# Linear attention's decay levels on half tiles: scaling on VectorE alone, and a predicated copy from PSUM in place of mask product and sum

## What is computed

```python
diff = bc[:, :, :, None, :] - bc[:, :, None, :, :]
decay = jnp.exp(jnp.where(causal[:, :, None], diff, -jnp.inf))
attn = jnp.einsum('bhid,bhjd,bhijd->bhij', qc, kc, decay)
o_intra = jnp.einsum('bhij,bhje->bhie', attn, vc)
```

## Time and profile before

| | us |
|---|---|
| median of 3 runs (907.64 to 909.5) | 908.16 |
| the profiled execution | 906.52 |
| its span in the trace | 904.7 |
| PE busy | 859.0 (95%) |
| DVE busy | 649.4 (72%) |
| ACT busy | 555.5 (61%) |
| POOL busy | 350.5 (39%) |

### The profile page before, as it was taken

One profiled execution on the slowest core, in us unless ns is written; L12 is line 12 of the kernel. 1 busy time (PEld: TensorE's weight loads), 2 busy tenths in 40 slices (PEclk: granted clock), 3 DMA queues, 4 the chain that ended last, 5 costly groups with the idle time before them and its releaser, 6 DMA issues.

```text
span 904.7 us, 18066 instructions
## 1 busy us (share of the span) xinstructions
PE 859.0 (95%) x6762; PEld 837.4 (93%) x6762; DVE 649.4 (72%) x1059; ACT 555.5 (61%) x999; POOL 350.5 (39%) x324
## 2 busy tenths in 40 slices
PE   4999889999999999999999989899999999999996
PEld 3998889999899899999999878799999999999996
DVE  5987999896777798777665659957577854444542
ACT  5677778887646576665555675456645655555441
POOL 3799995435432253333110215701032243333111
PEclk9999999999999999999999999999999999999999
DMA  5655444444565366665656443245345466654741
GB/s 201 209 187 186 162 144 151 137 132 140 151 184 186 111 189 205 186 180 175 214 163 194 160 142 110 82 136 166 115 143 172 150 211 188 182 180 152 217 133 47
DMA packets 42310, 146.41 MB, mean 162 GB/s; under 512 B 4704, under 2 KB 7024, under 8 KB 42224
## 3 DMA queue, kind: packets, MB, share of 16 engines
q1 hardware_dynamic: 41472, 143.67, 50.9%
q10 hardware_dynamic: 752, 1.59, 0.5%
HBM read 144.20 MB, written 1.05 MB: 161 GB/s over the span
## 4 chain that ended last, share of the span: by engine, by line
PE 72%; DVE 11%; issue 8%; POOL 6%; ACT 3%; DMA 1%; DVEq 0%; POOLq 0%; ACTq 0%
PE px L507 22%; PE px L508 22%; PE px L509 22%; DVE wlo L1316 3%; POOL CA L1876 2%; DVE px L1375 2%; POOL att L1996 1%; PE px L549 1%; PE px L571 1%; ACT whi L843 1%; DVE sq L1331 1%; POOL wlo L1827 1%; DVE Q L1406 1%; DMA X<-xs 1%; ACT hx L870 1%
## 5 line engine op out<-in xcount | busy, mean ns | idle before, releaser
L507 PE MATMUL px<-hx,whi 128*128 128x256 f32 x1392 | 404.4, 291 | 9.2 <-DVE hx L1337 6.1
L509 PE MATMUL px<-hx,wlo 128*128 128x256 f32 x1392 | 396.6, 285 | 0.0
L508 PE MATMUL px<-hx,whi 128*128 128x256 f32 x1392 | 396.6, 285 | 0.0
L1316 DVE TENSOR_TENSOR wlo<-raw,whi 128x1024 fp32r<-128x1024 f32 x251 | 330.8, 1325 | 65.0 <-ACT whi L843 64.6
L843 ACT ACTIVATE whi<-raw 128x1024 fp32r<-128x1024 f32 x267 | 279.9, 1051 | 65.0 <-PE px L509 49.8
L507 PEld LDWEIGHTS px<-hx,whi 128*128 128x128 f32 x1392 | 269.7, 194 | 14.2 <-DVE hx L1337 7.4
L508 PEld LDWEIGHTS px<-hx,whi 128*128 128x128 f32 x1392 | 270.0, 194 | 0.4
L509 PEld LDWEIGHTS px<-hx,wlo 128*128 128x128 f32 x1392 | 269.7, 194 | 0.0
L1950 POOL TENSOR_TENSOR fx<-tt,fx 128x256 fp32r<-128x256 f32 x40 | 54.3, 1359 | 130.1 <-ACT fx L1104 130.1
L1876 POOL TENSOR_TENSOR CA<-CA,ct 128x256 f32<-128x256 f32 x90 | 85.7, 953 | 45.5 <-ACT ct L910 37.9
L508 PE MATMUL px<-fx,whi 128*128 128x256 f32 x352 | 99.6, 283 | 0.0
(11 more groups left out here) (283 smaller groups left out, 1347.0 us busy)
## 6 DMA issues: line engine op xcount, KB each, us to landing
raw<-ws SPq DMA_DIRECT2D x267, 512.0 KB, 3.7
tb<-tabs SPq DMA_DIRECT2D x16, 128.0 KB, 2.7
out<-X SPq DMA_DIRECT2D x4, 256.0 KB, 2.4
X<-xs SPq DMA_DIRECT2D x1, 512.0 KB, 4.9
X<-xs ACTq DMA_DIRECT2D x1, 512.0 KB, 5.0
msk<-lmask ACTq DMA_DIRECT2D x1, 448.0 KB, 3.5
vc<-vecs ACTq DMA_DIRECT2D x1, 320.0 KB, 7.0
ug<-pos ACTq DMA_DIRECT2D x1, 128.0 KB, 4.7
```

What stands on the lines that cost most here:

```text
L507: e.matmul(b[:, 0:S], H, xh, start=first, stop=False)
L508: e.matmul(b[:, 0:S], H, xl, start=False, stop=False)
L509: m = e.matmul(b[:, 0:S], L, xh, start=False, stop=end)
L1316: e.tensor_tensor(wlo[:, n % NSL, :], raw[:, n % NRAW, :], whi[:, n % NSL, :], ALU.subtract).then_inc(s_lov, 1)
```

## The change

`factors` on DVE is now two instructions of half the size, border minus b left of the border and b minus border right of it, so both are negative and ACT needs one exp (scale +1/16) and no absolute value. Keys are scaled only left of each border and queries only right of it, both on DVE; the queries are packed into 128x256. The products then have 64 columns (the right-half queries) instead of 128. Level 0 is as before. For the other levels a predicated copy from PSUM writes the wanted places of `at` directly, two of 128x256; mask product, `tmp` and sum go. POOL loses all its level work and gets two memsets of `kL` and of half of `go`. The mask shrinks from 7x128 to 128 + 6x64 columns.

```diff
@@ TensorE, products(n), n > 0
-                    e.wait_ge(s_ql, n)
-                    e.wait_ge(s_kl, n)
+                    e.wait_ge(s_ql, n)
-                        m = e.matmul(bs[par][:, i * P:i * P + P], k_[o:o + 64, p_, t * P:t * P + P],
-                                     q_[o:o + 64, p_, t * P:t * P + P], start=(i == 0), stop=True, skip_group_check=True)
+                            m = e.matmul(bs[par][:, i * 64:i * 64 + 64], KL[n % 2][o:o + 64, p_, t * P:t * P + P],
+                                         QLf[n % 2][o:o + 64, i * 64:i * 64 + 64], start=(i == 0), stop=True,
+                                         skip_group_check=True)
@@ TensorE, linear_out()
-                e.wait_ge(s_la, 12)
+                for par in range(2):
+                    e.wait_ge(*BANK["pr", 6, par])
@@ ScalarE, factors(n)
-                e.activation(E, E, ACT.Abs).then_inc(s_fa, 1)
-                e.wait_ge(s_fa, n)
-                e.activation(E, E, ACT.Exp, scale=-1.0 / 16).then_inc(s_fe, 1)
+                e.activation(E, E, ACT.Exp, scale=1.0 / 16).then_inc(s_fe, 1)
@@ VectorE
-                if n > 2:
-                    e.wait_ge(s_kl, n - 2)
-                e.tensor_tensor(eb[:, n % 2, :].rearrange("p (n w) -> p n w", w=2 * s), bv,
-                                bv[:, :, s - 1:s].to_broadcast([P, 512 // (2 * s), 2 * s]), ALU.subtract).then_inc(s_fs, 1)
+                e.tensor_tensor(to_first, border, first, ALU.subtract)
+                e.tensor_tensor(to_second, second, border, ALU.subtract).then_inc(s_fs, 1)
...
-                e.tensor_tensor(QLf[n % 2], gqf, eb[:, n % 2, :], ALU.mult).then_inc(s_ql, 1)
+                e.tensor_tensor(halves(KLf[n % 2], n)[0], halves(gkf, n)[0], first, ALU.mult)
+                e.tensor_tensor(QLf[n % 2][:, 0:S].rearrange("p (n w) -> p n w", w=s), halves(gqf, n)[1], second,
+                                ALU.mult).then_inc(s_ql, 1)
...
-                    e.tensor_tensor(to[:, par, :].rearrange("p (a i) -> p a i", a=4), bt, mb, ALU.mult).then_inc(
-                        BANK["pr", n, par][0], 1)
+                        to = at[:, par, :].rearrange("p (a n w) -> p a n w", a=4, w=2 * s)[:, :, :, s:2 * s]
+                        e.copy_predicated(to, mb.to_broadcast([P, 4, 64 // s, s]),
+                                          px_of["pr", n, par][:, 0:S].rearrange("p (a n w) -> p a n w", a=4, w=s)).then_inc(
+                                              BANK["pr", n, par][0], 1)
@@ GpSimd
+            for n in range(2):
+                e.memset(KLf[n], 0.0).then_inc(s_pad, 1)
...
-                e.tensor_tensor(KLf[n % 2], gkf, eb[:, n % 2, :], ALU.mult).then_inc(s_kl, 1)
...
-                    e.tensor_tensor(at[:, par, :], at[:, par, :], tmp[:, par, :], ALU.add).then_inc(s_la, 1)
```

More of the change, by code:

```diff
@@ L10 @@
 I32 = mybir.dt.int32
+U32 = mybir.dt.uint32
 ALU = mybir.AluOpType
@@ L410, in two_blocks @@
         s_pad = sem("s_pad")
[L412 to L413 removed]
+        s_fs, s_fe, s_ql, s_pr, s_dec, s_dk, s_tk, s_cu, s_go = (sem(n) for n in (
+            "s_fs", "s_fe", "s_ql", "s_pr", "s_dec", "s_dk", "s_tk", "s_cu", "s_go"))
         s_gsq, s_gsm, s_gr, s_ogt, s_gn, s_gg, s_gph, s_gpv, s_gpg = (sem(n) for n in (
@@ L705, in products @@
                         p_, t = i // 2, i % 2
-                        m = e.matmul(bs[par][:, i * P:i * P + P], k_[o:o + 64, p_, t * P:t * P + P],
-                                     q_[o:o + 64, p_, t * P:t * P + P], start=(i == 0), stop=True, skip_group_check=True)
+                        if n == 0:
+                            m = e.matmul(bs[par][:, i * P:i * P + P], gk[o:o + 64, p_, t * P:t * P + P],
+                                         gq[o:o + 64, p_, t * P:t * P + P], start=(i == 0), stop=True,
+                                         skip_group_check=True)
+                        else:
+                            m = e.matmul(bs[par][:, i * 64:i * 64 + 64], KL[n % 2][o:o + 64, p_, t * P:t * P + P],
+                                         QLf[n % 2][o:o + 64, i * 64:i * 64 + 64], start=(i == 0), stop=True,
+                                         skip_group_check=True)
                 m.then_inc(s_pr, 1)
@@ L1141, in _ @@
             e.dma_start(caus[:, :], tabs[NH]).then_inc(s_caus, 16)
-            e.dma_start(msk[:, :, :], masks.rearrange("p (l i) -> p l i", l=7)).then_inc(s_msk, 16)
+            e.dma_start(msk[:, :], masks).then_inc(s_msk, 16)
             for n, key in enumerate((("cq", 0), ("cq", 1), ("cq", 2), ("ckv", 0))):
@@ L1689, in level_add @@
                     e.wait_ge(s_msk, 16)
[L1690 to L1696, removed]
-                    e.tensor_tensor(to[:, par, :].rearrange("p (a i) -> p a i", a=4), bt, mb, ALU.mult).then_inc(
-                        BANK["pr", n, par][0], 1)
+                    mb = msk[:, 0:P].rearrange("p (a i) -> p a i", a=1).to_broadcast([P, 4, P])
+                    for par in range(2):
+                        e.tensor_tensor(at[:, par, :].rearrange("p (a i) -> p a i", a=4),
+                                        px_of["pr", 0, par][:, :].rearrange("p (a i) -> p a i", a=4), mb,
+                                        ALU.mult).then_inc(BANK["pr", 0, par][0], 1)
+                else:
+                    s = LEVELS[n]
+                    mb = msk[:, P + 64 * (n - 1):P + 64 * n].bitcast(U32).rearrange("p (a n w) -> p a n w", a=1, w=s)
+                    for par in range(2):
+                        e.wait_ge(*BANK["pr", n - 1, par])
+                        to = at[:, par, :].rearrange("p (a n w) -> p a n w", a=4, w=2 * s)[:, :, :, s:2 * s]
+                        e.copy_predicated(to, mb.to_broadcast([P, 4, 64 // s, s]),
+                                          px_of["pr", n, par][:, 0:S].rearrange("p (a n w) -> p a n w", a=4, w=s)).then_inc(
+                                              BANK["pr", n, par][0], 1)
             def linear(key):
@@ L2074, in shape_constants @@
     j, i = np.arange(P)[:, None], np.arange(P)[None, :]
[L2075 to L2080, removed]
+    ms = [(j == i).astype(np.float32)]
+    for s in LEVELS[1:]:
+        m = (j // (2 * s) == i // (2 * s)) & (j % (2 * s) < s)
+        ms.append(m[:, i[0] % (2 * s) >= s].astype(np.float32))
+    ms = np.concatenate(ms, 1)
     half = np.arange(16, dtype=np.float32) / np.float32(16)
@@ L2086, in shape_constants @@
     over, shift = (np.where(cosine, np.pi / 2, v).astype(np.float32) for v in (100.0, 0.0))
-    return tabs, ms.reshape(P, 7 * P), inv[q % 16], sgn, over, shift
+    return tabs, ms, inv[q % 16], sgn, over, shift
 def kernel(**inputs):
```

48 lines of the change are left out of this document (15 added, 33 removed).

## The result

The changed kernel takes **898.68 us** (median of 4 runs, 895.31 to 899.27), the kernel before beside it 907.97 (907.64 to 909.5): a ratio of **0.9889, 95% interval 0.9871 to 0.9907** (the two medians alone give 0.9898). The forecast was 899.5, the range 895.0 to 903.5. Two executions at a much lower clock, one of experiment 8 (932.87 us) and one of the kernel before beside experiments 1 to 4 (1184.97), stand outside all ratios here. The profiled execution after is 898.74 us with a span of 896.9, against 906.52 and 904.7 before.

What follows compares the result with a forecast made beforehand. PE was taken as the bound, delayed by POOL directly and through DVE: 8.27 us of pauses, less 0.9 staying, plus 1.3 for the low clock, is 8.7. From the median 908.16 that gives 899.5 us, range 895 to 903.5.

Steps and rivals of the forecast that it cites:

- The bound: Between 535 and 600 us, PE's pauses, 8.27 us together, were put down to POOL's own time and its slowing of DVE.
- Level 1: Before level 1's products, PE's pause of 1.55 us goes, to within 0.1; keys and queries on DVE end at 540.75.
- Level 2: Before level 2's products, a pause of 0.9 us stays, of 1.90; DVE's queue lets PE start at 546.75.
- Level 3 and after: From level 3 on, pauses of 2.10 (level 5), 1.47 (key transpose), 0.92 (chunk sums) and 0.33 us (output) go.
- The products: On PE at levels 1 to 6, 64 columns instead of 128 bring no gain: 1.61 us a level.
- Rival B: Products of levels 1 to 6 do get cheaper with 64 columns, 0.80 us a level: 895.5 us; chance 10%.
- The copy: Each predicated copy on DVE takes 0.41 us, high end 1.22; two are 0.7 a level against 1.2 for mask products.
- Rival C: In the levels PE waits partly for DVE, copies at 1.22 us: 2 to 4 us lost, 902 to 904; chance 14%.
- Rival E: Predicated copies on DVE become the bound from 1.73 us each; at 2.4 they cost 8 us: 916; chance 5%.
- Rival D: The time goes to another wait, PE standing for late weights (`wlo`): 908 us, within 0.2%; chance 5%.
- The sum: Over the levels, 8.27 us of pauses, less 0.9 left at level 2, plus 1.3 for the low clock: 8.7 us.
- The step that failed: Outside the levels, no stretch was to change by more than a microsecond; otherwise the forecast is wrong.

Runs made afterwards that it cites:

- experiment 8: Changed kernel with level 2's factors and level 0's masks put ahead of level 1's scaling in DVE's queue: 898.15 us, ratio 0.989 against the kernel before.
- experiment 1: Kernel before with only the predicated copy in place of mask product and POOL's sums; keys stay on POOL: 903.18 us, ratio 0.9956.
- experiment 2: Kernel before with only the keys' scaling moved from POOL to DVE, at full width, ahead of the queries: 906.45 us, ratio 0.9983.
- experiment 3: Changed kernel with ACT's second pass, the absolute value, put back: 898.55 us, ratio 0.9912 against the kernel before.
- experiment 4: Changed kernel with 128 columns streamed in each product of levels 1 to 6, the upper 64 unused: 898.07 us, ratio 0.9908 against the kernel before.
- experiment 5: Changed kernel with each predicated copy preceded by another of the same size into unused `tmp`: 900.12 us, ratio 0.9928 against the kernel before.
- experiment 10: Changed kernel with POOL adding one unread 128x512 tile to itself after each copy: 899.46 us, ratio 0.9893 against the kernel before.
- experiment 12: Changed kernel with POOL adding two different unread 128x512 tiles after each copy: 901.35 us, ratio 0.9934 against the kernel before.

## Why the prediction was right, and where its steps were off

**The bound.** PE's losses in the levels, and POOL behind them: right. The copy alone, which takes POOL's sums away, gives 6.5 us of the stage, the keys on DVE alone 1.5, both with the halves and the single pass 10.2. The remaining 3.7 us between experiment 1 and the changed kernel are 0.7 for ACT's pass, 0.44 for the columns, 0.09 for the engine of the keys; the other 2.4 no run takes apart. They lie nearly all at levels 1 and 2, and the likeliest to make them are the shorter scalings (POOL 0.98 for 1.78), which isn't shown.

**Level 1.** Keys and queries were to end 4.89 us after level 0's products began (540.75 - 535.86); they end 4.93 after (544.68 - 539.75). The pause is gone, as forecast.

**Level 2.** Its products were forecast 10.89 us after level 0's (546.75 - 535.86); measured 10.87 (550.62 - 539.75), with an idle time of 0.77 for 0.9. It was read from DVE's queue, term by term, and experiment 8 shows that the queue was the cause. The agreement looks closer than it is: the forecast's terms add up to 5.97 us and an end at 546.72, not 546.6, and DVE took 5.79 (544.68 to 550.47), so by its own terms the step was 0.12 us out.

**Level 3 and after.** No pause, as forecast; transposes, chunk sums and output start undelayed. The low clock in the stage went: 1.00 in 569.5 to 573.

**The products.** Forecast without gain; measured 0.11 us a level (experiment 4), and 0.6 in all from the kernel before (1.61 or 1.64 a level there, 1.50 or 1.53 here). Rival B wanted 0.80 a level and falls (4.8 for six). By the Trainium skill (TensorE: Matmul & The Clock Gate, LDWEIGHTS) the load costs its 128 columns whatever is streamed. Experiment 4, 1.57 against 1.68 us, agrees far better with that than with the gap rule; in size a record's 0.094 us from start to start (1.50 / 16) lies below the page's 107 ns for a load.

**The copy.** Forecast 0.41; it is 0.43 to 0.45 at four levels and 0.73 to 0.80 at the last two, which no step foresaw. There DVE has room. The short runs of factors and scalings, costed at nothing, did cost nothing: 0.41 to 0.43 us at every level. Rival C was right as a mechanism: at 0.99 us a copy on average (experiment 5) 1.7 us are lost, in the last two places and not at the levels. Rival E's account gave the start of the chunk sums to 1.1 us at 2.71 us a copy; for the whole time it was 4.5 us short (11.8 for 16.3). Rival D had nothing: PE is at work throughout 535 to 590 but for 0.77 us.

**The sum.** 8.7 us forecast for the stage, 10.2 measured (forecast end near 589 when begun at 535.86, that is 53.1 us; measured 52.0). The terms that were too small: the bracketed idle times are shorter than the loss on PE, since from matmul start to matmul start the six places of before come to 9.93 us, less 1.08 for undelayed steps 8.85, not 8.27 (0.6); the products (0.6); the low clock, which costs 1.5 and not 1.3 (level 5 to level 6 was 6.18 us and is 4.60, less 0.08 for the products), 0.2; level 2's rest, 0.84 for 0.9. Together 1.4 of the 1.5; the last 0.1 I can't name.

**The step that failed** is the last of the list: no stretch outside the levels was to change by more than a microsecond. Both traces have 6762 matmul records, and matched one by one they show the changed kernel 3.9 us *later* when level 0's products begin, and 1.5 us ahead of its stage's gain after 682 us; 3.9 - 10.2 - 1.5 = -7.8, the difference of the executions. Windows of the kernel before:

```profile
151.00:158.00 7.00, 7.00 (x56) 6.85 (x56) 6.92 (x17) 5.69 (x16) 3.51 (x4) 1.00 0.46 122
132.60:136.00 3.40, 3.40 (x18) 3.40 (x17) 3.37 (x8) 0.00 (x0) 3.26 (x3) 0.50 0.24 65
310.00:314.00 4.00, 4.00 (x23) 4.00 (x23) 2.59 (x8) 1.20 (x2) 0.73 (x1) 0.57 0.00 1
681.50:686.00 4.50, 4.50 (x28) 4.50 (x27) 1.95 (x3) 1.76 (x3) 0.00 (x0) 0.62 0.62 212
```

and of the changed one:

```profile
151.00:158.00 7.00, 6.31 (x28) 6.16 (x29) 6.86 (x21) 1.24 (x2) 2.77 (x2) 0.51 0.41 114
...
132.60:136.00 3.40, 3.40 (x29) 3.37 (x28) 3.37 (x10) 0.30 (x1) 3.27 (x3) 1.00 0.15 43
...
681.50:686.00 4.50, 4.50 (x40) 4.50 (x39) 4.08 (x6) 3.31 (x6) 1.45 (x2) 1.00 0.60 216
```

Followed from matmul to matmul, the changed kernel is 0.7 us later at 97 us, gains 1.5 at 132.6, where it keeps its full clock, and by 158 us has lost 5.3: at 151 it waits 2.99 us for DVE and then runs at 0.51 for 6.8 us. Where the kernel before has its low stretch at 310 it gains 1.5, loses 0.9 by 322, and gains 1.5 at 682. In all that code the two kernels are the same, but for a smaller mask transfer and the two memsets at 493 us. Among the fourteen traced executions level 0's products begin anywhere between 535.3 and 542.3 us, and the low stretches fall now here, now there. So it was partly luck that the median came within 0.8 us of the forecast: 1.5 us too little was summed for the stage, while the traced execution gave back some of its gain outside.

The traces show what makes the pause at 151 us. The kernel before has 0.54 us of waiting there. In the changed one PE comes 0.74 us earlier and DVE 1.71 later, which makes 2.99. DVE loses its time between 144 and 147.5 us, beside POOL:

```profile
144.05 0.68 DVE L1421 TENSOR_SCALAR mx<-mx 128x2 f32<-128x2 f32 x1
...
145.85 1.77 DVE L1316 TENSOR_TENSOR wlo<-raw,whi 128x1024 fp32r<-128x1024 f32 x1
...
151.69 1.62 PE L550 MATMUL px<-K,Q 128*128 128x256 f32 x4 [2.99 <-DVE mx L1418]
```

In the kernel before the first takes 0.17 us and the second 1.22. All fourteen traces divide the same way. The five without a low stretch at 132 to 136 us (the changed kernel and experiments 3, 8, 10, 12) have these long DVE rows (0.68, and 1.76 or 1.77), a pause of 2.57 to 2.99 us at 150 to 152 us, and a low stretch from there on. The nine with one (it begins at 132.6 to 136.1) have 1.22 for the chunk and a pause of 0.52 to 0.55. So keeping the full clock at 133 us puts PE ahead and DVE's work beside POOL's, and the gain is lost again 15 us later, whichever kernel it is. What decides about the stretch at 133 us these runs don't show.

## What to carry to other kernels

Follow the queue of the engine that PE waits for, instruction by instruction, with durations free of contention: the two steps worked out so came within 0.04 and 0.12 us. Sum delays from matmul start to matmul start, not from the brackets. And judge a change of under 1% by its own stage in the trace as well as by the whole time: 0.8 us of experiment 8 and 0.7 of experiment 3 are plain in the stage and lost in the medians. And lay several traces side by side before a pause far from the edit is put down to chance: a gain of 1.5 us at one place here brings a loss at the next.

## What the runs showed of the hardware

- A predicated copy of 128x256 from PSUM takes 0.43 to 0.45 us, about as a plain copy (0.41 to 0.42); into gapped output runs of 2 or 1 elements it takes 0.73 to 0.80, while the plain copy stays at 0.41 to 0.42.
- POOL's adds of 128x512 take 1.04 us each (2.22 from start to end of a pair) when both inputs are one tile, and 1.28 or 1.29 (2.71) with two; single ones took up to 1.83 and 2.08. The second kind takes DVE's 256-element products from 0.42 to 1.32 and 1.50 us.
- An operation of 128x2 on DVE, 0.17 us by itself, took 1.53 to 2.12 us in five traces when it began inside a POOL pass of 2.35 to 2.53 us (near 151 us), and ended 0.02 to 0.04 us after that pass.
- A stretch of 3.4 us at a granted clock of 0.50 costs PE 1.5 us (133, 310, 570 and 682 us of the kernel before). Such stretches followed pauses of PE of 2.10 us (level 5 before), 2.99 (151 us after, for 6.8 us) and 0.88 (level 3 of experiment 12), yet pauses of 1.47 to 1.90 us in the earlier trace rows passed without one. The length of the pause alone doesn't tell.
- A record of a float32 matmul with a load of 128 columns costs 0.10 us whether 64 or 128 columns are streamed (from start to start 0.094 to 0.096 and 0.101 to 0.103; as rows of 16, 1.57 and 1.68 us).
